# The last down projection with feed-forward tiles stationary: tokens on rows, x turned by transposes, last norm by row sums

## The reference

```
for l in range(DEPTH):                     # DEPTH = 2
    ...                                    # attention and convolution branches, merged, added to x
    h = rmsnorm(x, ffn_norm_g[l])
    up = causal_dwconv(h @ w_ffn_up[l], ffn_dw_w[l], ffn_dw_b[l])     # D_FF = 2816, width 3
    gt, val = jnp.split(up, 2, axis=-1)
    x = x + (jax.nn.silu(gt) * val) @ w_ffn_down[l]
return rmsnorm(x, final_norm_g)            # x * rsqrt(mean(x*x) + EPS) * g
```

## Time and profile before

| | |
|---|---|
| three runs | 826.07, 826.69 and 826.80 us, median 826.69 |
| profiled execution | 827.24 us, of which the traced span is 825.4 |
| PE busy | 808.1 us (98%) |
| DVE, ACT, POOL busy | 588.8, 518.8, 456.7 us |
| PE granted clock, mean | 0.997 |

### The profile page before, as it was taken

How to read it: one execution, slowest core, us unless ns; L and a number is a source line. 1 busy time by engine, 2 the same in 40 slices (tenths; PEclk the granted TensorE clock), 3 DMA queues, 4 the chain that set the end, 5 groups by cost and what they waited for, 6 DMA issues and landing times.

```text
span 825.4 us, 16620 instructions
## 1 busy us (share of the span) xinstructions
PE 808.1 (98%) x6820; PEld 790.5 (96%) x6820; DVE 588.8 (71%) x1162; ACT 518.8 (63%) x852; POOL 456.7 (55%) x140
## 2 busy tenths in 40 slices
PE   8999999999999999999999999999999999999996
PEld 7999989899999999999999999989999999999995
DVE  5799998583559766666579999876535887665664
ACT  6856798773665655555576587887446654554543
POOL 6898787687722233222289987887875032223220
PEclk9999999999999999999999999999999999999998
DMA  8654444445455655555455544444454456545521
GB/s 288 212 204 148 161 151 150 154 155 189 169 172 185 205 187 177 199 170 188 154 197 168 198 154 154 154 145 151 165 194 165 157 202 204 202 155 201 179 81 52
DMA packets 21386, 142.26 MB, mean 172 GB/s; under 512 B 2624, under 2 KB 3136, under 8 KB 4672
## 3 DMA queue, kind: packets, MB, share of 16 engines
q1 hardware_dynamic: 20592, 140.43, 49.5%
q10 hardware_dynamic: 720, 0.78, 0.3%
HBM read 140.15 MB, written 1.05 MB: 171 GB/s over the span
## 4 chain that ended last, share of the span: by engine, by line
PE 78%; ACT 9%; DVE 8%; issue 2%; DMA 1%; POOL 1%; SPq 0%; DVEq 0%; ACTq 0%
PE pu L1034 21%; PE pu L1035 20%; PE pu L1036 20%; ACT whi L315 4%; DVE wlo L894 3%; PE ps L1034 2%; PE ps L1036 2%; PE ps L1035 2%; DVE pc L749 2%; ACT qk L563 1%; PE pt L1036 1%; PE pt L1035 1%; PE pt L1034 1%; DMA x<-in_x_t 1%; DVE gate L941 1%
## 5 line engine op out<-in xcount | busy, mean ns | idle before, releaser
L253 POOL TENSOR_TENSOR wlo<-raw,whi 128x2048 fp32r<-128x2048 f32 x86 | 397.3, 4624 | 334.0 <-ACT whi L315 333.8
L1034 PE MATMUL pu<-uh,whi 128*128 128x256 f32 x880 | 249.8, 284 | 1.8 <-POOL wlo L253 1.4
L315 ACT ACTIVATE whi<-raw 128x2048 fp32r<-128x2048 f32 x129 | 245.7, 1906 | 8.3 <-PE pu L1036 7.3
L1035 PE MATMUL pu<-ul,whi 128*128 128x256 f32 x880 | 249.0, 283 | 0.0
L1036 PE MATMUL pu<-uh,wlo 128*128 128x256 f32 x880 | 249.0, 283 | 0.0
L1034 PE MATMUL pu<-hh,whi 128*128 128x256 f32 x704 | 201.6, 286 | 2.2 <-POOL wlo L253 1.4
L1035 PE MATMUL pu<-hl,whi 128*128 128x256 f32 x704 | 199.1, 283 | 0.0
L1036 PE MATMUL pu<-hh,wlo 128*128 128x256 f32 x704 | 199.1, 283 | 0.0
L1034 PEld LDWEIGHTS pu<-uh,whi 128*128 128x128 f32 x880 | 168.9, 192 | 2.4 <-issue 2.3
L1035 PEld LDWEIGHTS pu<-ul,whi 128*128 128x128 f32 x880 | 168.9, 192 | 0.1
L1036 PEld LDWEIGHTS pu<-uh,wlo 128*128 128x128 f32 x880 | 168.9, 192 | 0.0
(11 more groups left out here) (210 smaller groups left out, 1232.9 us busy)
## 6 DMA issues: line engine op xcount, KB each, us to landing
raw<-in_weights SPq DMA_DIRECT2D x130, 1024.0 KB, 4.9
raw<-in_weights SPq DMA_DIRECT2D x3, 512.0 KB, 8.8
x<-in_x_t SPq DMA_DIRECT2D x2, 256.0 KB, 4.8
raw<-in_weights SPq DMA_DIRECT2D x2, 256.0 KB, 3.9
x<-in_x_t SPq DMA_DIRECT2D x1, 512.0 KB, 8.0
out_y<-qk SPq DMA_DIRECT2D x2, 256.0 KB, 2.8
out_y<-qk ACTq DMA_DIRECT2D x2, 256.0 KB, 2.7
par_all<-in_params SPq DMA_DIRECT2D x1, 236.0 KB, 6.9
```

Of the source, the lines that this page charges most:

```text
L253: nc.gpsimd.tensor_tensor(wlo[s][:, :], raw[s][:, :], whi[s][:, :].bitcast(f32), ALU.subtract).then_inc(lo_ready[s], 1)
L315: A(whi[s][:, :], raw[s][:, :], ACT.Copy).then_inc(hi_ready[s], 1)
L1034: MM(out, whi[s][:, w], hi, start=start, stop=False, skip_group_check=accumulate)
L1035: MM(out, whi[s][:, w], lo, start=False, stop=False, skip_group_check=accumulate)
```

## The change

In the second (last) layer alone, the down projection changes sides: a 128x128 piece of a hidden tile (128 hidden channels x 128 tokens) is stationary and 512 columns of down weights move (`row_product`). The four banks hold pieces b = 0 to 3 with tokens on rows: token tile b // 2, channel half b % 2. To x, which has channels on rows, 16 transposes are applied (`turn_x`, in steps 1 and 2, into banks po and pu1, both free then), ACT copies the result to x_rows (in the tile cv), and DVE adds it to the banks in steps 4 to 7 (before PE's down unit of that step, which waits for it). The last down unit begins with the first of its two hidden tiles. The final norm's sums of squares are then along rows: ACT squares with a running sum. The gain lies along the columns and is loaded once more to every partition. The root is one value per row. Output is written with tokens on rows in four transfers. POOL has nothing to do at the end any more.

```diff
+                def row_product(b, s, ab, tile):
+                    tokens, w = slice(P * (b // 2), P * (b // 2) + P), slice(D_MODEL * ab + 512 * (b % 2), D_MODEL * ab + 512 * (b % 2) + 512)
+                    high, low = fh[:, tile, tokens], fl[:, tile, tokens]
+                    MM(down_rows[b], high, whi[s][:, w], start=False, stop=False, skip_group_check=True)
+                    MM(down_rows[b], low, whi[s][:, w], start=False, stop=False, skip_group_check=True)
+                    return MM(down_rows[b], high, wlo[s][:, w], start=False, stop=True, skip_group_check=True)
+                def turn_x(token_tile):
+                    pe.wait_ge(x_copied, l * 4 + 4)
+                    if token_tile:
+                        pe.wait_ge(x_rows_kept, 2 * token_tile)
+                    for half, bank in enumerate((po, pu[1])):
+                        places = bank[:, :, :].rearrange("p a (b t) -> p (a b) t", t=P)
+                        for n in range(4):
+                            last = nc.tensor.transpose(places[:, n, :], x[:, 4 * half + n, P * token_tile:P * token_tile + P], ident)
+                    last.then_inc(x_turned, 1)
...
@@ PE, ffn_step @@
-                    unit(0, n + 11, uh, ul)
+                    unit(0, n + 11, uh, ul, None, {(1, 0): lambda: turn_x(j - 1)} if l == DEPTH - 1 and j <= 2 else {})
+                    if l == DEPTH - 1 and 4 <= j < 8:
+                        pe.wait_ge(x_rows_added, j - 3)
                     down_unit(1, k - 2, 1 - parity)
...
@@ PE, last down unit of the last layer @@
+                    for b, ab in ((0, 0), (1, 0), (0, 1), (1, 1), (2, 0), (2, 1), (3, 0), (3, 1)):
+                        if b == 0:
+                            hidden_split(ab)
+                        last = row_product(b, 2, ab, ab)
...
@@ ACT, ffn_step, after hidden_high(k, 0, parity) in steps 1 and 2 @@
+                    for half, bank in enumerate((po, pu[1])):
+                        A(x_rows[:, 2 * token_tile + half, :], bank[:, :, :].rearrange("p a t -> p (a t)"), ACT.Copy).then_inc(x_rows_kept, 1)
@@ ACT, before the squares of the output projection @@
+                if l == DEPTH - 1:
+                    act.dma_start(gate[:, 1, 0:4, :].rearrange("p n t -> p (n t)"), gf_in.partition_broadcast(P)).then_inc(gf_in_s, 16)
@@ DVE, ffn_step, after hidden_low(k - 1, 1, 1 - parity), in steps 4 to 7 @@
+                        V.tensor_tensor(down_rows[b], down_rows[b], x_rows[:, b, :], ALU.add).then_inc(x_rows_added, 1)
...
@@ ACT, the end @@
+            for b in range(4):
+                A(square_rows[b], down_rows[b], ACT.Square, accum_out=row_sums[:, b:b + 1]).then_inc(row_sum, 1)
...
+                if b % 2 == 0:
+                    A(part, row_sums[:, b:b + 1], ACT.Identity, scale=1.0 / D_MODEL, bias=const[:, C_EPS:C_EPS + 1]).then_inc(row_part, 1)
+                else:
...
+                    A(log, row_sums[:, b:b + 1], ACT.Ln, scale=1.0 / D_MODEL, bias=part).then_inc(row_log, 1)
...
+                    A(root, log, ACT.Exp, scale=-0.5).then_inc(row_root, 1)
+            act.wait_ge(y_gained, 1)
+            A(y_rows[:, 3, :], down_rows[3], ACT.Copy, scale=row_roots[:, 1:2]).then_inc(y_last, 1)
@@ DVE, the end @@
+            normalised(0)
+            normalised(1)
+            dve.wait_ge(row_sum, 4)
+            V.tensor_tensor(down_rows[3], down_rows[3], gains[:, 1, :], ALU.mult).then_inc(y_gained, 1)
+            normalised(2)
```

More of the change, by code:

```diff
@@ L138, in hybrid_encoder @@
         down = [ps[0], ps[1], pt, pc]
+        down_rows = [bank[:, :, :].rearrange("p a t -> p (a t)") for bank in down]
+        x_rows = cv[:, :, :].rearrange("p (b n) t -> p b (n t)", b=4)
+        gains = gate[:, 1, 0:4, :].rearrange("p (b n) t -> p b (n t)", b=2)
+        square_rows = [tile[:, :, :].rearrange("p a t -> p (a t)") for tile in (kvraw, kr, vwin, probs[0])]
+        row_sums, row_parts = sb("row_sums", [P, 4]), sb("row_parts", [P, 2])
+        row_logs, row_roots = sb("row_logs", [P, 2]), sb("row_roots", [P, 2])
         angles = ps[0][:, 0, :]
@@ L238, in _ @@
                         load_unit(s, slice(r * RING + s, r * RING + s + 1))
[L240 to L243, removed]
+            for b in range(3):
+                sp.wait_ge(y_ready, b + 1)
+                sp.dma_start(y_out[:, b, :], y_rows[:, b, :]).then_inc(y_out_s, 16)
+            sp.wait_ge(y_out_s, 16 * 4)
         @block.gpsimd
@@ L600, in _ @@
                         split_high(l, s, USES)
[L601 to L605, removed]
-                        gained_high(l + 1, i, down[i][:, :, :])
[L607 to L611, removed]
@@ L612, in _ @@
-                if l < DEPTH - 1:
+                    for i in range(4):
+                        act.wait_ge(x_ready, l * 8 + 4 + i + 1)
+                        A(po[:, :, :] if i == 0 else sq[:, 2 * i:2 * i + 2, :], down[i][:, :, :], ACT.Square).then_inc(sq_ready, 1)
+                        gained_high(l + 1, i, down[i][:, :, :])
                     split_high(l, 2, USES)
                     next_high(l + 1, U_GLU)
-                else:
-                    keep_quarters(pu[0][:, 0, :], l * 1 + 2)
@@ L993, in _ @@
                 hidden_low(k0 + FT - 1, 1, 0)
[L995 to L1013, removed]
-                if l < DEPTH - 1:
+                if l < DEPTH - 1:
+                    for i in range(4):
+                        if i < 3:
+                            dve.wait_ge(down_done, l * 3 + i + 1)
+                        else:
+                            dve.wait_ge(unit_done[2], l * USES + USES)
+                        if i == 0:
+                            dve.wait_ge(x_copied, l * 4 + 4)
+                        V.tensor_tensor(down[i][:, :, :], down[i][:, :, :], x[:, 2 * i:2 * i + 2, :], ALU.add).then_inc(x_ready, 1)
+                        if i:
+                            gained_low(l + 1, i - 1)
                     gained_low(l + 1, 3)
@@ L1018, in _, with normalised @@
                         V.tensor_copy(x[:, 2 * i:2 * i + 2, :], down[i][:, :, :]).then_inc(x_kept, 1)
[L1020 to L1024, removed]
+            def normalised(b):
+                dve.wait_ge(row_root, b // 2 + 1)
+                V.scalar_tensor_tensor(y_rows[:, b, :], down_rows[b], row_roots[:, b // 2:b // 2 + 1], gains[:, b % 2, :],
+                                       ALU.mult, ALU.mult).then_inc(y_ready, 1)
+            dve.wait_ge(gf_in_s, 16)
+            normalised(0)
[3 more added lines that the diff above has]
+            normalised(2)
         @block.tensor
@@ L1296, in down_unit @@
                         tile = 2 * parity + ab
-                        for m in range(NT):
+                        for m in range(NT if l < DEPTH - 1 else 0):
                             last = product(down[m // 2][:, m % 2, :], s, NT * ab + m, fh[:, tile, :], fl[:, tile, :], False, True, True)
+                        for b in range(4 if l == DEPTH - 1 else 0):
+                            last = row_product(b, s, ab, tile)
                     last.then_inc(unit_done[s], 1)
@@ L1316, in _, with hidden_split @@
                 pe.wait_ge(lo_ready[2], lo_count(2, (l + 1) * USES - 1))
[L1318 to L1332, removed]
+                def hidden_split(ab):
+                    pe.wait_ge(fh_ready, (l + 1) * FT - 1 + ab)
+                    pe.wait_ge(fl_ready, (l + 1) * FT - 1 + ab)
+                if l < DEPTH - 1:
+                    pe.wait_ge(fh_ready, (l + 1) * FT)
+                    pe.wait_ge(fl_ready, (l + 1) * FT)
+                    for i in range(4):
+                        for m in (2 * i, 2 * i + 1):
+                            for ab in range(2):
+                                last = product(down[i][:, m % 2, :], 2, NT * ab + m, fh[:, ab, :], fl[:, ab, :], False, True, True)
+                        if i < 3:
+                            last.then_inc(down_done, 1)
+                        else:
+                            last.then_inc(unit_done[2], 1)
+                else:
+                    for b, ab in ((0, 0), (1, 0), (0, 1), (1, 1), (2, 0), (2, 1), (3, 0), (3, 1)):
+                        if b == 0:
+                            hidden_split(ab)
+                        last = row_product(b, 2, ab, ab)
+                        if ab and b < 3:
+                            last.then_inc(down_done, 1)
+                    last.then_inc(unit_done[2], 1)
 def kernel(**inputs):
@@ L1403 @@
     y = r.results[0]["out_y"]
-    return np.ascontiguousarray(y.transpose(2, 1, 0)).reshape(1, SEQ, D_MODEL)
+    return np.ascontiguousarray(y.reshape(P, SEQ // P, D_MODEL).transpose(1, 0, 2)).reshape(1, SEQ, D_MODEL)
```

40 lines of the change are left out of this document (27 added, 13 removed).

## The result

| | before | changed |
|---|---|---|
| median of four runs | 826.62 us | 820.09 us (819.96 to 820.79) |
| ratio | | 0.9922, 95% interval 0.9911 to 0.9934 |
| profiled execution, and its span | 827.24, 825.4 | 820.79, 819.0 |

The change makes the kernel 6.5 us faster. The forecast was 817.3 with a range of 815.9 to 820.7; what came is the time of rival 1, 820.1. It lies outside the forecast's own range (816.2 to 818.5), and inside the wide one only because that one adds rival 1, which had a chance of 14%.

The account below looks back on a forecast made before the run. PE, 98% busy, was taken as the bound, then the serial tail. PE -5.31 (-6.34 + 1.76 - 0.30 - 0.43) and tail -4.06 gave -9.37: 826.69 to 817.3 us; own range 816.2 to 818.5, eight-in-ten 815.9 to 820.7.

Parts of the forecast that it names:

- rival 1: Down passes: fixed fp32r price per pass, 0.227 us instead of 0.216; +2.6 to 2.8, 820.1 us; chance 14%.
- reading (a): Down passes: extra 12 ns go with the weight load, hidden under 512 cycles; 0.216 us a pass, 6.34 us saved.
- (b): Down passes: extra 12 ns are a fixed price of each fp32r pass; 0.227 us, 0.31 saved per unit.
- The turned x: Steps 1 and 2: sixteen transposes of x in PE's stream at 0.11 us each, +1.76.
- The wait at 659: Step 2: PE waits 0.33 us for DVE's low split; arriving 0.30 late there costs nothing, -0.30.
- The last unit: Last down unit: starting on the first of two hidden tiles removes PE's wait for the last, -0.43 us.
- The tail: From PE's last data to last output issue: 6.17 us falls to 2.11, -4.06.
- 2: Down passes: no saving per pass, 0.24 us each; only 3.1 us gained, 823.6 us; chance 6%.
- 3: Down passes: a wide fp32r pass is worse than two narrow ones; at half rate +48 us, 874; chance 4%.
- 4: Down passes: PE and loads overlap beyond the stream, pitch 0.12 whatever the width; 25 us less, 792; chance 1%.
- 5: Middle steps: faster PE meets the splits and waits, taking ten steps' saving; +5.5, 822.8 us; chance 3%.
- 6: Kernel end: tail dearer by 1 to 2 us, from a serial arm or late ACT; 818.8 us; chance 7%.

Follow-up runs that it names:

- first program of bare passes: Separate program of matmuls alone on one core, not a kernel variant; fp32r passes stood at 0.227, 0.175 and 0.119 us with 512, 384 and 256 columns.
- narrow version: The changed kernel with each down pass of 512 columns cut into two of 256; 823.48 us, ratio 0.9961 to the kernel before.
- version without x: The changed kernel without the transposes of x, their copies and additions, so x is missing from the last sum; 819.21 us.
- bfloat16 version: The changed kernel with the two small passes of each three in the last down projection in bfloat16, ACT making bfloat16 copies; 822.97 us.

## Why the prediction came out 2.8 us low

**The passes: the step that failed.** "Price 0.216: 24 passes are 5.18 us" was reading (a), and it measured 0.227: 5.46 a unit. The reading was that the 12 ns of the narrow pass "goes with the longer load, and under 512 cycles that load has been seen hidden". The rows behind it were true, but they compared types as well as loads: the plain float32 passes with the same load of 192 ns are not fp32r. The first program of bare passes shows the 13 ns at 512 columns just as at 256, in fp32r alone. The term was mis-sized: 11 x (5.76 - 5.453) = 3.4 us and not 6.34, 3.0 less, which is the whole miss and a little more. That wide passes save per pass is shown by the narrow version. The mechanism (fewer, wider passes on a PE that is never idle, and a shorter tail) was right, and so was (b) as the way in which it could fail, with 0.227 and 820.1 in figures; it got its 14% by the same mixed rows. Its count of 216 passes leaves out the last unit's 24.

**The turned x.** 1.76 on PE forecast; eight transposes measured 0.87, so 1.74. The wait at 659: forecast that PE arrives there late by 0.30 with 0.33 to give. With the true price of the down unit (0.31 less, not 0.58 less) it arrives 0.56 late, and no wait is left; without the transposes it is back, at 0.63. Without a wait the two up units of step 2 are 0.39 shorter (11.91 before, 11.52 less the transposes), not 0.30.

**The last unit.** The wait of 0.43 is gone, as forecast; without the early start it would be 0.71 now.

**PE in all.** With the measured terms the prediction's sum is -3.38 + 1.74 - 0.39 - 0.43 = -2.46 and not -5.31. Measured, from 630 on: the last pass starts 185.26 - 182.68 = 2.58 earlier, and as its slot is 0.107 longer, it ends 2.47 earlier.

**The tail.** Forecast 6.17 to 2.11; measured 2.27. Of the two arms DVE's was the longer by 0.17 (the gain's product ends at 814.83, the root at 814.66), as the sum had it. On it the last copy took 0.69 and not 0.60 and began 0.10 behind the product and not 0.03: that is the 0.16. The logarithm took 0.29 and not 0.20, off this path. Copy and logarithm read a value per partition as scale or bias, which the forecast's rows did not; the root, which reads none, took its 0.20; no run takes this difference apart. From the end of PE's last slot to the end of the span it was 10.0 before and is 5.8 (813.22 to 819.0). So of the 6.4 us between the two traced spans 4.2 are the tail's and 2.47 PE's, less 0.27 by which the stretch happened to start later.

**Copies, additions, gains: nothing**, as priced; the version without x shows it for the first two. No run leaves out the load of the gains. No PE wait stands in the steps.

**The rivals.** 1 is what came. 2 is the narrow version's time, 823.5. Nothing came of 3, 4 and 5, and of 6 only 0.16. The bfloat16 version shows how far 5 was: even 2.7 us of added work a step on ACT bring waits only in step 2 and at the last tile.

## What to carry to other kernels

A pass with fp32r operands and a full load costs its columns at 2.4 GHz plus some 13 ns, with 256 columns as with 512 (a granted clock of 1.00 in all these stretches); so turning a product so that 512 columns move is worth 13 ns for each pair of passes, and pays only where the transposes that the turned layout needs (0.11 us each) cost less than it saves, as at the end of a kernel, where it also makes a norm's sums fall along rows and shortens the tail by 4 us. When an unseen form is priced from neighbours, the neighbour has to share its type: one bare run of passes would have settled it. A moved wait is best read between two fixed points of PE's stream, which here repeats to a hundredth of a microsecond, and not from whole times.

## What the runs showed of the hardware that I had not expected

- fp32r has a nearly fixed price per pass, 12 to 15 ns over the columns at 2.4 GHz: 0.119, 0.175, 0.227 us with 256, 384, 512 columns; bfloat16 0.109 and 0.216. With 128 columns fp32r takes 0.112, bfloat16 0.056, so this price doesn't hold for narrow passes.
- Passes of both types one after another keep almost the price of fp32r: 0.676 to 0.68 for a triple whose parts alone are 0.659. What in the array causes it stays open.
- With 64 stationary columns the price of fp32r was half at 256 columns (0.113), whole at 384 (0.173) and more at 512 (0.230). Open too.
- The Trainium skill ("TensorE: Matmul & The Clock Gate", Back-to-back issue gap) has 131 ns as the sustained distance with 512 columns; no run here with 512 columns came below 216 ns, the isolated gap of the same section, and the runs here decide. The 275 ns for a transpose in a kernel (the same page, Part 4: PE-mode transpose) is here the length of one (272), while eight of them took 0.87 us of PE. The granted clock stayed at 1.00 over them; as they last under 1 us between other passes, that doesn't test what the section says of transposes and the clock.
